# Running norms with another order, two norms joined, two modulation chunks and the forget gates' sums at other places

## The chip, the cores and the metric

The kernel runs on one core of a Trainium2 chip, in one launch. The metric is device time in microseconds. A core has TensorE (PE, matmuls), VectorE (DVE), ScalarE (ACT), GpSimd (POOL) and SyncE (SP, which here issues nearly all DMAs). Each engine works off its own queue in order, and the kernel orders them among each other by semaphores alone.

## The reference

Two blocks in a row, on 512 latent tokens of 1024 channels, and 256 context tokens in all but the last layer of the first block. All data is float32. Cut to what the change touches:

```python
def layer_norm(x, g, b):
    mu = jnp.mean(xf, axis=-1, keepdims=True)
    var = jnp.mean(jnp.square(xf - mu), axis=-1, keepdims=True)
    return (xf - mu) * lax.rsqrt(var + NORM_EPS) * g + b
...
for l in range(DEPTH):                                   # first_block, DEPTH = 2
    sh1, sc1, g1, sh2, sc2, g2 = split(silu_c @ w_mod[l] + b_mod[l], 6)
    a_lat = x_lat * (1 + sc1) + sh1
    m_lat, m_ctx = mixer(a_lat, a_ctx, ...)
    x_lat = layer_norm(ALPHA * x_lat + (1 + g1) * m_lat, ln1_g[l], ln1_b[l])
    f_lat = swiglu(x_lat * (1 + sc2) + sh2, ...)
    x_lat = layer_norm(ALPHA * x_lat + (1 + g2) * f_lat, ln2_g[l], ln2_b[l])
...
h = modulate(rms_norm_2(x, norm_mix), shift_m, scale_m)  # second_block, on x_lat
x = x + gate_m * hybrid_mixer(h, ...)                    # log_f = log_sigmoid(f_c + fox_bf); cum = cumsum(log_f)
h = modulate(rms_norm_2(x, norm_ffn), shift_f, scale_f)
x = x + gate_f * hierarchical_moe(h, ...)
```

After the last layer of the first block a layer norm and the second block's RMS norm follow each other with nothing between.

## The kernel before, in words

**Layout.** The stream x lies in SBUF with channels on the 128 partitions: 8 tiles of 128 channels, each 768 tokens wide (512 in layer 1). Sums over channels are matmuls with a matrix of ones.

**Dense pieces.** All large products go through `run_dense`. A piece is 128 output channels. SP loads its weights (`w_raw`, 8 or 11 blocks of 128x128), ACT rounds them to `w_hi` (L1217), DVE forms the rest `w_lo` (L1227), and PE adds w_hi by hi, w_lo by hi (L1200, L1201) and w_hi by lo (L1203). `w_raw`, `w_hi` and `w_lo` have two buffers each, so SP issues the load for piece n when w_lo of piece n-2 is done, and ACT casts it when PE has ended piece n-2. Per piece n every engine first prepares piece n+1, then does the background work registered for n (`behind`), then takes piece n's output. SP issues the load of a piece first and then the background work of the piece before.

**Background: modulation vectors.** `Vectors` computes silu(c) by w_mod beside a run of pieces: chunks of 512 columns, each in 4 steps. A step loads a quarter of the rows (`vec_w`, 512 KB, L930, two buffers; the next load waits until DVE has used the buffer), and DVE adds it up (L950, L953: 4 instructions for two vectors). Per chunk ACT and DVE split the sum (`vec_hi`, `vec_lo`, L979, L938) and PE puts it into a row of PSUM (L989). `start` is the piece at which it begins, `pieces` the number of pieces per chunk. In layer 0's projection (20 pieces) it computes 8 chunks, 2 pieces each, from piece 4: all vectors from column 2D on. In layer 0's feed-forward part (60 pieces) it computes layer 1's 12 chunks, 4 pieces each, from piece 2.

**Bias tables.** In the projections POOL gathers relative-position biases by 24 small DMAs in three groups of 8 (L1981) into a landing area and subtracts them from a mask (L1984).

**Norms.** A running norm (`Norm` with `running=True`) has its sums gathered while the dense layer in front still works: `Moments` centres x roughly (L1359), ACT squares it (L1371), POOL adds tiles up (L1378, L1382) and PE totals them (L1335). At the norm's start PE adds the last tile (L611), ACT makes minus the mean (L640), DVE and POOL subtract it (L736, 3 tiles; L750, 5 tiles), ACT loads the table with the square root and takes the root (L652, L654), DVE takes the reciprocal (L743) and multiplies (L768), ACT applies gain and modulation twice (L667: the rounded `ahi`, then the full value), and DVE forms `alo` (L773). Three norms are of this kind: both of layer 0 at width 768, and layer 1's first at 512. PE's first matmuls (L1178, L1179) interleave the first two pieces, so they need both their `w_lo` and one `ahi` tile at a time; L1184 follows with `alo`. The last norm of the first block is another function, `normalize`, in a block of its own: POOL has added the first seven tiles (L1305), PE sums (L486), DVE centres (L537), ACT squares and PE sums again (L502, L491), DVE, ACT and DVE make the reciprocal root (L540, L504, L542), DVE multiplies (L554) and ACT applies gain and bias (L515). The second block's norm then squares again (L649, L623), makes its own root (L758, L663, L760), and goes on as L768, L667, L773.

**Second block's projection.** 16 pieces with `Branches` behind them: convolution, gates, and the forget gates: softplus on DVE, a running sum `fox_cum` on DVE in piece 5 (L2769), then in piece 6 PE turns it (L2659) and spreads it over partitions (L2663), ACT copies it to `fox_ck` (L2705), DVE to `fox_cq` (L2776), and POOL makes the decay tables (L2827, L2831).

## Time and profile before

| what | us |
|---|---|
| median of 3 runs (lowest, highest) | 3197.33 (3195.94, 3199.88) |
| profiled execution: time | 3194.6 |
| profiled execution: span of the core | 3192.8 |
| PE busy | 2899.0 (91%) |
| DVE, ACT, POOL busy | 1684.6, 1231.2, 485.9 |
| mean granted TensorE clock | 0.953 |

The span reaches from the first to the last instruction of the core; the time of the execution has a little around it. "Busy" leaves out waiting. An engine that waits is followed by the name of what released it; a wait for several things is put down to the last of them. A granted clock of 1.00 is TensorE's upper level, 0.50 its lower.

### The profile page before, as it was taken

What the parts mean: (1) busy time and instruction counts of PE and PEld (TensorE: products, weight loads), DVE (VectorE), ACT (ScalarE), POOL (GpSimd) and SP (SyncE); (2) the same over time, 40 slices, a digit from 0 to 9 for tenths busy, and PEclk for the clock granted to TensorE, in tenths of its full rate; (3) what the DMA queues carried; (4) which work ended last, traced back from release to release, by engine and by line L of the source; (5) the groups of instructions that cost most, each with busy time, mean ns of one, the idle gap of its engine ahead of it and who ended that gap; (6) DMA issues with size and microseconds to landing.
All of it is one profiled execution on the core that took longest, in us unless ns stands there. A gap on an engine that the chain in (4) does not pass through costs nothing. (4 is left out here: it accounts for less than half of the span.)

```text
span 3192.8 us, 37028 instructions
## 1 busy us (share of the span) xinstructions
PE 2899.0 (91%) x14711; PEld 2304.0 (72%) x14711; DVE 1684.6 (53%) x2345; ACT 1231.2 (39%) x1827; POOL 485.9 (15%) x437
## 2 busy tenths in 40 slices
PE   7898899999979999999798799998999968876995
...
GB/s 208 150 185 32 24 1 38 62 70 60 52 40 131 128 122 107 120 91 41 99 60 16 24 10 99 99 83 114 190 165 190 93 32 81 159 76 192 371 241 79
DMA packets 397871, 330.11 MB, mean 103 GB/s; under 512 B 38038, under 2 KB 340484, under 8 KB 397572
## 3 DMA queue, kind: packets, MB, share of 16 engines
...
q10 hardware_dynamic: 256, 0.07, 0.0%
...
## 5 line engine op out<-in xcount | busy, mean ns | idle before, releaser
L1200 PE MATMUL ps<-ahi,w_hi 128*128 128x512 f32 (+1 forms) x2264 | 769.0, 353 | 11.2 <-DVE w_lo L1227 11.2
L1201 PE MATMUL ps<-ahi,w_lo 128*128 128x512 f32 (+1 forms) x2264 | 768.0, 353 | 0.0
L1227 DVE TENSOR_TENSOR w_lo<-w_raw,w_hi 128x1024 fp32r<-128x1024 f32 (+2 forms) x241 | 341.4, 1417 | 377.2 <-ACT w_hi L1217 375.3
L1200 PEld LDWEIGHTS ps<-ahi,w_hi 128*128 128x128 f32 x2264 | 428.9, 189 | 78.3 <-DVE w_lo L1227 14.6
L1203 PE MATMUL ps<-alo,w_hi 128*128 128x512 f32 (+1 forms) x2264 | 473.2, 351 | 0.0
L1217 ACT CAST w_hi<-w_raw 128x1024 fp32r<-128x1024 f32 (+2 forms) x244 | 285.7, 1171 | 485.3 <-PE ps L1203 368.4
L1201 PEld LDWEIGHTS ps<-ahi,w_lo 128*128 128x128 f32 x2264 | 429.0, 189 | 60.7 <-issue 0.2
L1203 PEld LDWEIGHTS ps<-alo,w_hi 128*128 128x128 f32 x2264 | 376.4, 189 | 58.0
L953 DVE SCALAR_TENSOR_TENSOR vec_acc<-vec_w,csilu,vec_acc 128x512 f32<-128x512 f32 x364 | 257.3, 752 | 8.3 <-DMA vec_w<-in_w_mod 3.6
L1290 DVE SCALAR_TENSOR_TENSOR x<-ps,mod,x 128x512 f32<-128x512 f32 x80 | 51.4, 668 | 241.8 <-PE ps L1203 226.9
L1378 POOL TENSOR_TENSOR xsum<-x 128x768 f32<-128x768 f32 (+1 forms) x3 | 5.1, 1692 | 1058.4 <-DVE x L1359 1058.4
L1200 PE MATMUL ps<-hhi,w_hi 128*128 128x512 f32 (+1 forms) x462 | 156.9, 354 | 0.0
L1201 PE MATMUL ps<-hhi,w_lo 128*128 128x512 f32 (+1 forms) x462 | 156.5, 353 | 0.0
L3342 ACT CAST e_hi<-e_raw 128x2048 fp32r<-128x2048 f32 x69 | 131.6, 1912 | 15.9 <-DMA e_raw<-in_w_up 9.7
L1898 POOL TENSOR_SCALAR prob<-prob,nm 128x512 f32<-128x512 f32 (+3 forms) x64 | 79.7, 1245 | 371.1 <-DVE nm L1823 371.1
L1452 ACT CAST hhi<-hf 128x768 fp32r<-128x768 f32 (+1 forms) x44 | 32.0, 727 | 268.6 <-DVE hf L1460 268.6
L1534 DVE TENSOR_TENSOR gp<-sg,ps 128x768 f32<-128x768 f32 (+1 forms) x32 | 26.3, 821 | 196.5 <-PE ps L1203 179.4
L1525 ACT ACTIVATE sg<-ps 128x768 f32<-128x768 f32 (+1 forms) x48 | 33.8, 705 | 241.0 <-PE ps L1203 241.0
L1263 ACT COPY proj<-ps 128x512 f32<-128x512 f32 (+2 forms) x58 | 40.0, 756 | 179.0 <-PE ps L1203 168.7
L2199 PE MATMUL ps<-mla_pt,proj 128*128 128x512 f32 x192 | 102.5, 616 | 0.0
L1200 PEld LDWEIGHTS ps<-hhi,w_hi 128*128 128x128 f32 x462 | 86.7, 188 | 13.2
L1201 PEld LDWEIGHTS ps<-hhi,w_lo 128*128 128x128 f32 x462 | 86.7, 188 | 12.8
...
## 6 DMA issues: line engine op xcount, KB each, us to landing
vec_w<-in_w_mod SPq DMA_DIRECT2D x128, 512.0 KB, 3.8
...
```

The costliest lines, as they stand in the source:

```text
L953: m = dve.scalar_tensor_tensor(out=acc, in0=w, scalar=f, in1=acc, op0=ALU.mult, op1=ALU.add)
L1200: pe.matmul(o, whi[:, j, b0 + b, :], hi[:, b, t0:t0 + tn], start=(b == 0), stop=False)
L1201: pe.matmul(o, wlo[:, j, b0 + b, :], hi[:, b, t0:t0 + tn], start=False, stop=False)
L1203: m = pe.matmul(o, whi[:, j, b0 + b, :], lo[:, b, t0:t0 + tn], start=False, stop=(b == nb - 1))
L1217: act.copy(whi[:, j, 0:d.blocks, :], raw_of(d, i, jj)).then_inc(hi_ready[j].sem, 1)
L1227: dve.tensor_tensor(wlo[:, j, 0:d.blocks, :], raw_of(d, i, jj), whi[:, j, 0:d.blocks, :].bitcast(F32), ALU.subtract).then_inc(lo_ready[j]. ...
L1263: m = act.copy(o_, s_) if scale is None else act.activation(o_, s_, ACT.Identity, scale=scale)
L1290: m = dve.scalar_tensor_tensor(out=xo, in0=ps[:, b + t0:b + t0 + tn], scalar=mod[:, v, bass.ds(i * 2 + (gate + jj), 1)], in1=xo, op0=ALU.m ...
L1525: act.activation(sg[:, jj, :], ps[:, 4 * BANK * jj:4 * BANK * jj + T], ACT.Sigmoid).then_inc(gated.sem, 1)
L1898: pool.tensor_scalar(self.prob[:, j, slot, 0:u.keys], self.prob[:, j, slot, 0:u.keys], self.nm[:, j, slot, 3:4], None, ALU.mult).then_inc( ...
L2199: m = pe.matmul(ps[:, bank:bank + LAT], weight(b, j), self.pt[:, s % 3, :], start=(b == 0), stop=(b == kt - 1))
L3342: act.copy(whi[:, n % HI, :], raw[:, n % RAW, :]).then_inc(e_hi.sem, 1)
```

## The change

Four edits.

1. In the three running norms the load of the table with the root moves to the end of the block before (`Moments.act`, at p == KT). ACT casts the first two weight pieces after the root instead of one before and one after it. DVE makes both `w_lo` after the first multiply; before, it made one ahead of the reciprocal, and POOL made the other between its subtractions.
2. `normalize` is gone. The last layer uses `Moments`, as the others do, and `DoubleNorm` computes layer norm and RMS norm in one block: it subtracts and multiplies, takes squares of gain times x plus bias on ACT, sums them on PE, applies gain and bias in place (6 tiles on DVE, 2 on ACT), takes the second root, and goes on as before. POOL makes both first `w_lo`.
3. In layer 0's projection `Vectors` computes 6 chunks from piece 8 on. The remaining 2 (the gate of the feed-forward part, from column 5D) come in layer 0's feed-forward part, in front of layer 1's 12 chunks, at 3 pieces per chunk instead of 4, in the same buffers.
4. The forget gates' turn and spread (PE), copies (ACT, DVE) move from piece 6 to piece 8.

```diff
-        def normalize(tiles, T, eps, gain, bias=None, center=False, post=None, after=None, src=None, presum=None):
...
-                    if center:
-                        dve.wait_ge(norm_mean.sem, norm_mean.base + 1)
-                        for k in range(n):
-                            dve.scalar_tensor_tensor(out=tiles[k], in0=ps[:, 0:T], scalar=-1.0 / dim, in1=src[k],
-                                                     op0=ALU.mult, op1=ALU.add).then_inc(norm_c.sem, 1)
-                    dve.wait_ge(norm_var.sem, norm_var.base + n)
-                    dve.tensor_scalar(rstd[:], ps[:, 1024:1024 + T], 1.0 / dim, eps, ALU.mult, ALU.add).then_inc(norm_rstd.sem, 1)
-                    dve.wait_ge(norm_sqrt.sem, norm_sqrt.base + 1)
-                    ch.link(dve.reciprocal(rstd[:], rstd[:]))
...
             def act_root(self, act):
-                act.activation(warm[:], ones[:, 0:1], ACT.Sqrt)
+                if self.tail:
+                    act.activation(warm[:], ones[:, 0:1], ACT.Sqrt)
                 act.wait_ge(*self.sem(norm_rstd, 1))
                 act.activation(self.rstd, self.rstd, ACT.Sqrt, bias=0.0 if self.tail else ln_eps[:]).then_inc(norm_sqrt.sem, 1)
 
-            def act_apply(self, act):
+            def act_apply(self, act, halves=None):
                 hi = self.post[0]
+                if self.running:
+                    halves(0)
+                    halves(1)
...
-                    if k == self.ON_DVE + 2:
-                        split(pool)
                     pool.tensor_tensor(self.src[k], self.src[k], self.sq[1], ALU.add).then_inc(norm_c.sem, 1)
...
                     if self.running and k == 0:
+                        halves(0)
+                        halves(1)
                         self.recentred(dve, 2)
...
+        class DoubleNorm(Norm):
...
+            def pe(self, pe):
+                pe.matmul(self.sums, ones[:], self.src[self.n - 1], start=False, stop=True, skip_group_check=True).then_inc(norm_mean.sem, 1)
+                pe.wait_ge(*self.sem(norm_sq, 1))
+                pe.matmul(self.squares, ones[:], self.sq[0], start=False, stop=True, skip_group_check=True).then_inc(norm_var.sem, 1)
+                for k in range(self.n):
+                    pe.wait_ge(*self.sem(norm_sq, k + 2))
+                    pe.matmul(self.sum2, ones[:], self.sq[k % 2], start=(k == 0), stop=(k == self.n - 1), skip_group_check=True).then_inc(norm_var.sem, 1)
...
+            ON_ACT = 6
+
+            def act_apply(self, act, halves):
+                for k in range(self.n):
+                    act.wait_ge(*self.sem(norm_x2[0], k + 1))
+                    if k >= 2:
+                        act.wait_ge(*self.sem(norm_var, k))
+                    act.activation(self.sq[k % 2], self.src[k], ACT.Square, scale=self.gain1(k), bias=self.bias1(k)).then_inc(norm_sq.sem, 1)
...
+                halves(0)
+                act.wait_ge(*self.sem(norm_rstd, 3))
+                act.activation(self.rstd, self.rstd, ACT.Sqrt).then_inc(norm_sqrt.sem, 1)
+                halves(1)
+                for k in range(self.ON_ACT, self.n):
+                    affine(k)
...
+            def recentred(self, dve, k):
+                dve.tensor_tensor(self.src[k], self.src[k], self.rest, ALU.add).then_inc(norm_x2[1].sem, 1)
+
+            def pool(self, pool, split):
+                pool.wait_ge(*self.sem(norm_g, 1))
+                for k in range(self.ON_DVE, self.n):
+                    pool.tensor_tensor(self.src[k], self.src[k], self.rest, ALU.add).then_inc(norm_c.sem, 1)
+                split(pool, 0)
+                split(pool, 1)
...
+            def dve_apply(self, dve, halves):
+                lo = self.post[1]
+                dve.wait_ge(*self.sem(norm_rstd, 2))
+                for k in range(self.n):
+                    dve.wait_ge(*(self.sem(norm_x2[1], k + 1) if k < self.ON_DVE else self.sem(norm_c, k - self.ON_DVE + 1)))
+                    dve.tensor_tensor(self.src[k], self.src[k], self.rstd, ALU.mult).then_inc(norm_x2[0].sem, 1)
+                    if k == 0:
+                        self.recentred(dve, 2)
+                for k in range(self.ON_ACT):
+                    dve.wait_ge(*self.sem(norm_sq, k + 2))
+                    dve.tensor_scalar(self.src[k], self.src[k], self.gain1(k), self.bias1(k), ALU.mult, ALU.add).then_inc(norm_mean.sem, 1)
+                dve.wait_ge(*self.sem(norm_var, self.n + 1))
+                dve.tensor_scalar(self.rstd, self.sum2, 1.0 / self.dim, self.eps, ALU.mult, ALU.add).then_inc(norm_rstd.sem, 1)
+                dve.wait_ge(*self.sem(norm_sqrt, 2))
+                dve.reciprocal(self.rstd, self.rstd).then_inc(norm_rstd.sem, 1)
+                dve.wait_ge(*self.sem(norm_rstd, 4))
...
+                def scaled(k):
+                    dve.wait_ge(*(self.sem(norm_mean, 2 + k) if k < self.ON_ACT else self.sem(norm_g, 3 + k - self.ON_ACT)))
+                    if k >= 2:
+                        dve.wait_ge(*self.sem(norm_tmp, k - 1))
+                    dve.tensor_tensor(self.xn[k % 2], self.src[k], self.rstd, ALU.mult).then_inc(norm_x2[0].sem, 1)
+
+                scaled(0)
+                scaled(1)
...
-            def __init__(self, c, w, cols, first, bias, dst, pieces, start=0, norm_first=False):
+            def __init__(self, c, w, cols, first, bias, dst, pieces, start=0, norm_first=False, end=6 * D, room=None):
                 self.cols, self.first, self.bias, self.dst, self.nv = cols, first, bias, dst, len(cols)
-                self.chunks = (6 * D - first) // self.CN
+                self.chunks = (end - first) // self.CN
...
+                if room is None:
...
+                self.room = self.raw, self.acc, self.hi, self.lo = room
...
@@ -1364,6 +1335,8 @@
                     dve.wait_ge(*self.at(self.centred, k + 1))
 
             def act(self, act, p):
+                if p == KT:
+                    act.activation(warm[:], ones[:, 0:1], ACT.Sqrt)
                 for k in self.SQUARED.get(p, ()):
                     act.wait_ge(*(self.at(self.centred, k + 1) if k <= 3 else self.written(k)))
...
@@ -2501,7 +2474,7 @@
                         if l == 0:
                             prologue(g["w_mod"][0], (0, 1), vec2[:, 0:48], mod, ring, w_in, proj, bt)
                         landing = proj[:, T_CQ:T_CQ + 3, :].rearrange("p a t -> p (a t)")[:, 0:ROWS * HEADS * 32].rearrange("p (r h c) -> p r h c", r=ROWS, h=HEADS)
-                        vectors = () if l else (Vectors(c1, g["w_mod"][0], (0, 1), 2 * D, vec2[:, 0:48], mod, 2, start=4, norm_first=True),)
+                        vectors = () if l else (Vectors(c1, g["w_mod"][0], (0, 1), 2 * D, vec2[:, 0:48], mod, 2, start=8, norm_first=True, end=5 * D),)
                         g0, b0 = (V_LN2_G + (l - 1) * KT, V_LN2_B + (l - 1) * KT) if l else (V_LN_IN_G, V_LN_IN_B)
                         norm = Norm(c1, xt(ALL), ALL, LN_EPS, lambda k, m=1: col(vec1, g0 + k, m), (ahi, alo, *modulate_by(mod, 0)),
                                     [proj[:, T_NV + n, :] for n in range(2)], proj[:, T_NV + 2, :], [proj[:, T_NV + n, :] for n in (3, 0, 1)],
...
-                           Vectors(c1, g["w_mod"][l + 1], (0, 1), 0, vec2[:, (l + 1) * 48:(l + 2) * 48], later, 4, start=2, norm_first=True))
-                room = vectors.raw[:].rearrange("p a b c -> p (a b c)")
-                moments = None if last else Moments(T, [room[:, n * T:(n + 1) * T] for n in range(2)], temps[0][:])
+                if last:
+                    vectors = (Vectors(c1, g["w_mod_2"][0], (2,), 0, vec3[:, 0:48], later, 4, start=2, norm_first=True),)
+                    vectors[0].ended()
+                else:
+                    gates = Vectors(c1, g["w_mod"][l], (0, 1), 5 * D, vec2[:, l * 48:(l + 1) * 48], mod, 3, start=2, norm_first=True)
+                    gates.ended()
+                    vectors = (gates, Vectors(c1, g["w_mod"][l + 1], (0, 1), 0, vec2[:, (l + 1) * 48:(l + 2) * 48], later, 3, start=gates.end, room=gates.room))
...
-            if last:
-                normalize(xt(T), T, LN_EPS, lambda k: col(vec1, g2 + k), lambda k: col(vec1, b2 + k), center=True, after=ALPHA, presum=xsum)
+                run_dense(new_ring(c1, NH), layers, moments.pool,
+                          background=(*vectors, moments.of(layers)), norm=norm)
+                moments.ended()
...
                     for t in range(4):
                         m = pe.transpose(ps[0:FOX_H, 6 * BANK + t * P:6 * BANK + (t + 1) * P], self.soft[:, 4 * t:4 * t + 4], ident[:])
                     m.then_inc(soft_rows.sem, 1)
-                if n == 6:
+                if n == 8:
                     pe.wait_ge(cum_done.sem, 1)
                     for t in range(4):
...
                         act.activation(self.a0[:, k, :], self.r[:, k, :], ACT.Exp, scale=self.sc[:, k:k + 1]).then_inc(a_exp.sem, 1)
                     for k in range(2):
                         act.activation(self.tmp[:, k, :], self.r[:, k, :], ACT.Tanh, scale=self.sc[:, 2 + k:3 + k]).then_inc(a_exp.sem, 1)
-                if n == 6:
+                if n == 8:
                     for h in range(FOX_H):
                         act.wait_ge(ck_mm.sem, h + 1)
                         act.copy(self.ck[:, h, :], self.bank(h)).then_inc(ck_copied.sem, 1)
...
-                if n == 6:
+                if n == 8:
                     dve.wait_ge(cq_mm.sem, 1)
                     dve.tensor_copy(self.cq[:], ps[:, 7 * BANK:7 * BANK + 16].rearrange("p (t h) -> p t h", h=FOX_H)).then_inc(cq_copied.sem, 1)
+                if n == 6:
...
+                            g2, b2 = V_LN2_G + (DEPTH - 1) * KT, V_LN2_B + (DEPTH - 1) * KT
+                            norm = DoubleNorm(c2, xt(LAT), LAT, lambda k: col(vec1, g2 + k), lambda k: col(vec1, b2 + k), RMS_EPS,
+                                        lambda k, m=1: col(vec1, V_MIX + k, m), (ahi, alo, *modulate_by(mod, 0)),
```

The names in the order below: w_raw and w_hi, w_lo are weight pieces, vec_w the modulation weights, x the stream, rstd the reciprocal root; a number at a name's end tells tiles apart. First SP's queue at the start of layer 0's projection, before and then after:

```order
L1124 UNCONDITIONAL_BRANCH
L1139 DMA w_raw<-in_w_in 128x8x128 x4
L930 DMA vec_w<-in_w_mod 128x2x512 x2
L1139 DMA w_raw<-in_w_in 128x8x128
L930 DMA vec_w<-in_w_mod 128x2x512 x2
```
```order
L1108 UNCONDITIONAL_BRANCH
L1123 DMA w_raw<-in_w_in 128x8x128 x8
L915 DMA vec_w<-in_w_mod 128x2x512 x2
L1123 DMA w_raw<-in_w_in 128x8x128
L915 DMA vec_w<-in_w_mod 128x2x512 x2
```

Eight weight loads (pieces 2 to 9) now stand in a row ahead of the first modulation load, where four stood. Next DVE's queue from the end of the first block to the second block's first pieces, before and after (the pairs L768, L773 go on the same way):

```order
L1290 SCALAR_TENSOR_TENSOR x<-ps,mod_9,x 128x512 x2
L1103 UNCONDITIONAL_BRANCH
L517 UNCONDITIONAL_BRANCH
L537 SCALAR_TENSOR_TENSOR x<-ps,x 128x512 x8
L540 TENSOR_SCALAR rstd<-ps 128x512
L542 RECIPROCAL rstd<-rstd 128x512
L554 TENSOR_TENSOR sq<-x,rstd 128x512 x8
L471 UNCONDITIONAL_BRANCH
L1222 UNCONDITIONAL_BRANCH
L704 TENSOR_TENSOR norm_co<-vec_4,mod_8 128x8
L708 COPY norm_co<-mod_8 128x8
L1227 TENSOR_TENSOR w_lo<-w_raw,w_hi 128x1024 x2
```
```order
L733 TENSOR_TENSOR x<-x,tmp_159 128x512
L611 SCALAR_TENSOR_TENSOR rstd<-ps,tmp_158 128x512
L733 TENSOR_TENSOR x<-x,tmp_159 128x512
L630 RECIPROCAL rstd<-rstd 128x512
L747 TENSOR_TENSOR x<-x,rstd 128x512
L733 TENSOR_TENSOR x<-x,tmp_159 128x512
L747 TENSOR_TENSOR x<-x,rstd 128x512 x7
L752 TENSOR_SCALAR x<-x,vec_4 128x512 x6
L754 TENSOR_SCALAR rstd<-ps 128x512
L756 RECIPROCAL rstd<-rstd 128x512
L763 TENSOR_TENSOR xn<-x,rstd 128x512 x2
```

One block less; the eight subtractions from PSUM are now three here and five on POOL, and both `w_lo` are gone from DVE. Last PE's queue at the forget gates, before (between pieces 5 and 6) and after (between pieces 7 and 8):

```order
L1203 MATMUL ps<-a2lo,w_hi 128x512 x8
L2659 MATMUL ps<-ident,fox_cum 128x4 x4
L2663 MATMUL ps<-fox_cum,fox_sel 128x512 x4
L1200 MATMUL ps<-a2hi,w_hi 128x512
L1201 MATMUL ps<-a2hi,w_lo 128x512
```
```order
L1187 MATMUL ps<-a2lo,w_hi 128x512 x8
L2631 MATMUL ps<-ident,fox_cum 128x4 x4
L2635 MATMUL ps<-fox_cum,fox_sel 128x512 x4
L1184 MATMUL ps<-a2hi,w_hi 128x512
L1185 MATMUL ps<-a2hi,w_lo 128x512
```

The same eight instructions stand two pieces later.

## Rows read from the trace of the kernel before

**Rows 1.** Timeline of layer 0's projection: start us, us, engine, line, operation [idle before <-releaser].
```profile
107.69 1.12 PE L1203 MATMUL ps<-alo,w_hi 128*128 128x256 f32 x8
116.03 1.12 PE L1203 MATMUL ps<-alo,w_hi 128*128 128x256 f32 x8
126.46 4.00 SPq L930 DMA_DIRECT2D vec_w<-in_w_mod  x2
128.46 6.05 POOL L1981 DMA_DIRECT2D proj<-rpb_rows  x8 [0.32 <-POOL na_bias L1984]
130.50 0.47 SPq L1139 DMA_DIRECT2D w_raw<-in_w_in  x1
147.64 7.87 POOL L1984 TENSOR_TENSOR na_bias<-na_mask,proj 128x256 f32<-128x256 f32 x8 [13.13 <-DMA proj<-rpb_rows]
148.66 1.04 ACT L1217 CAST w_hi<-w_raw 128x1024 fp32r<-128x1024 f32 x1 [12.99 <-DMA w_raw<-in_w_in]
153.22 0.61 PE L989 MATMUL ps<-vec_hi,pick_row 128*16 128x512 f32 x1 [10.12 <-DVE vec_lo L938]
159.17 0.43 PE L1200 MATMUL ps<-ahi,w_hi 128*128 128x512 f32 x1
```
**Rows 2.** Timeline of the second block's projection, around the forget gates.
```profile
2663.51 1.04 ACT L1217 CAST w_hi<-w_raw 128x1024 fp32r<-128x1024 f32 x1 [11.55 <-DMA w_raw<-in_w_in]
2666.99 0.59 PE L2659 MATMUL ps<-ident,fox_cum 4*128 4x4 f32 x4 [11.19 <-DVE fox_cum L2769]
2667.44 7.17 PE L2663 MATMUL ps<-fox_cum,fox_sel 4*128 4x512 f32 x8
2678.12 0.47 PE L1200 MATMUL ps<-a2hi,w_hi 128*128 128x512 f32 x1
2693.32 0.59 ACT L1263 COPY proj<-ps 128x512 f32<-128x512 f32 x1 [1.69 <-PE ps L1203]
```
**Rows 3.** PE's timeline from layer 1's last matmuls to the second block's first.
```profile
2557.88 2.68 PE L1203 MATMUL ps<-hlo,w_hi 128*128 128x512 f32 x11
2585.51 9.37 PE L623 MATMUL ps<-sq,ones 128*128 128x512 f32 x16 [12.75 <-ACT sq L649]
2603.97 0.77 PE L1178 MATMUL ps<-a2hi,w_hi 128*128 128x512 f32 x1 [9.09 <-ACT a2hi L667]
```
**Rows 4.** DVE's timeline in the same two norms.
```profile
2572.80 0.69 DVE L540 TENSOR_SCALAR rstd<-ps 128x512 f32<-128x512 f32 x1 [4.27 <-PE ps L491]
2574.19 3.35 DVE L542 RECIPROCAL rstd<-rstd 128x512 f32<-128x512 f32 x1 [0.70 <-ACT rstd L504]
2602.21 1.29 DVE L768 TENSOR_TENSOR xn<-x,rstd 128x512 f32<-128x512 f32 x2
```
**Rows 5.** Timeline of layer 1's running norm, width 512.
```profile
2171.92 1.10 PE L611 MATMUL ps<-x,ones 128*128 128x512 f32 x2 [0.30 <-PEq L1103]
2174.42 0.69 DVE L724 SCALAR_TENSOR_TENSOR sg<-ps,hf 128x512 f32<-128x512 f32 x1
2178.30 0.70 ACT L654 ACTIVATE sg<-sg,ln_eps 128x512 f32<-128x512 f32 x1
2182.42 1.70 DVE L768 TENSOR_TENSOR x<-x,sg 128x512 f32<-128x512 f32 x1
```
**Rows 6.** Timeline of layer 0's first running norm, width 768; the last row is width 512's.
```profile
924.12 2.82 DVE L1227 TENSOR_TENSOR w_lo<-w_raw,w_hi 128x1024 fp32r<-128x1024 f32 x1
936.85 8.50 ACT L667 ACTIVATE ahi<-x,norm_co 128x512 fp32r<-128x512 f32 x14 [2.04 <-DVE x L768]
...
2187.52 5.04 ACT L667 ACTIVATE ahi<-x,norm_co 128x512 fp32r<-128x512 f32 x7 [2.54 <-DVE x L768]
```
**Rows 7.** Weight tiles in layer 0's feed-forward part: time to landing.
```profile
DMA to landing us min/median/max: 3.6/3.9/5.5
```
**Rows 8.** That part's busy times (columns PE, PEld, DVE, ACT, POOL), and modulation chunks.
```profile
955.00:1440.00 485.00, 484.81 (x2767) 421.47 (x2768) 261.93 (x330) 112.52 (x121) 0.00 (x0) 0.99 0.39 115
...
L953 DVE SCALAR_TENSOR_TENSOR vec_acc<-vec_w,csilu,vec_acc x364: 737/746/1234, 104.2 to 2486.1; 128x512 f32<-128x512 f32 x182
```

191 lines of the change are left out of this document (52 added, 139 removed).

## The prediction

> **What bounds the kernel now.** I read the page first: PE is busy 91% of the span (the small table), so only two things can move the time: what PE has to do, and the stretches in which it waits. I then asked for PE's waits around the four edited places, and read the instructions in order of time in those stretches. Four waits come out. In layer 0's input projection PE stands still once for 10.12 us, and the page's releaser is the split of a modulation chunk [rows 1]. In the second block's projection it stands still for 11.2 us until a running sum is there [rows 2]. Between the last matmul of layer 1's feed-forward part and the first matmul of the second block, the chain runs through two whole norms [rows 3, 4]. And each of the three running norms has a gap of 11 to 14 us (the ends of the low halves and the reciprocal in [rows 5, 6]). The reader is to see that in all four the instruction PE waits for has itself waited: for a DMA, for a queue in front of it, or for a table load.
>
> **Layer 0's projection (term 1).** The wait at 143.10 (153.22 less 10.12) ends with vec_lo, but that split stands behind w_lo, w_lo behind w_hi, and w_hi waited 12.99 us for a weight load [rows 1]. That load was issued at 130.50 and its cast could start only at 148.66: 18.2 us, against 3.9 us (median to landing) where nothing is in the way [rows 7]. POOL had issued eight gathers of relative biases from 128.46 on, whose result was there at 147.64, so the load was caught behind them. It was issued that late because SP runs its queue in order, and in front of it stood modulation loads that wait until DVE has used the buffer: the pair at 126.46 goes out only after 4.00 us. The change takes the modulation loads out of the first four pieces. A piece lasts 8.34 us here (107.69 to 116.03, [rows 1]). Counting by that pitch from the end of piece 5 at 117.1 (116.03 and 1.12), pieces 6 to 9 would end at 125.5, 133.8, 142.1 and 150.5. The same load (piece 9's, pieces counted from 0) then goes out when w_lo of piece 7 is done, at about 120.3, and is needed as w_lo at 142.1. With 18.2 us to land and 2.4 us of cast and split it is ready at 140.9. Piece 10's load, at about 128.7, needs to be ready at 150.5 and is at 149.3. So even at the worst landing that this trace shows both are in time. What goes: 10.12 us of waiting, and the slow clock behind it. From 153.22 to 159.17 matmuls follow each other at 0.427 us, at the lower level, against 0.228 elsewhere (eleven in 2.68 us) [rows 1, 3]: 14 of them, 2.8 us. Term 1: 13.0 us saved; bounds 14 and 0 (the wait simply moves).
> The two chunks taken out go into layer 0's feed-forward part. Their 8 PE matmuls are moved, not added. There DVE gets 14 chunks in steps of 3 pieces instead of 12 in steps of 4. PE was busy 484.8 of 485 us in that stretch and DVE 261.9 [rows 8]; two more chunks are 32 instructions by 0.75 us, 24 us. Less the twelve chunks (192 by 0.746) DVE's own work is 118.7 us for 30 pairs of pieces, 4.0 a pair. Let all of it and two steps (8 by 0.75) fall into one piece, with 1.3 us of waiting for ACT between: 11.3 us. It starts 1.1 us after PE has ended the piece before, and with ACT's cast (1.04, [rows 1]) and its own low half (1.2) the next w_lo is done at about 14.7. PE needs it two pitches on, at 16.7. I cost this at nothing, with 2 us of cover per such piece.
>
> **The joined norms (term 2).** Before: PE's last dense matmul ends at 2560.56, the next real one starts at 2603.97: 43.4 us [rows 3] (2557.88 and 2.68, to 2603.97). After, the sums of layer 1's norm are gathered during the last layer as in the other running norms, and one chain remains. I build it from the running norm at the same width (512), from PE's start B (2171.92, [rows 5]). B comes 2.0 us after the last dense matmul, because two sums (twice the 1.10 us of this row) come first, as before that norm. DVE has the variance at B+3.2 and the second subtraction at B+4.15; the root ends at B+3.95, now without table load. Reciprocal 3.35: B+7.5. First multiply beside POOL 1.70, third subtraction 0.7, then seven multiplies by 0.70: DVE is through at B+15. Squares for the second norm start at B+9.3, PE's sums at B+10.1. Eight of them took 9.37 us in the old block [rows 3], so the sum stands at B+19.5. From variance to first multiply is 4.8 us and from there to PE's first matmul 1.76 us (2572.80 to the reciprocal's end, 2602.21 to 2603.97, [rows 3, 4]): PE starts at B+26.1. Casts, affine steps and POOL's two low halves lie beside the sums and the reciprocal. 2.0 + 26.1 = 28.1 instead of 43.4: 15.3 us saved. Against it stands one more pair of matmuls in the dense stream, 0.9 to 1.1 us [rows 5]. Term 2: 14.4 us; the DVE multiplies bound it: all eight at the contended 1.70 instead of 0.70 would give back 7, none contended would add 1, so 7 to 15.5.
>
> **The three running norms (term 3).** At width 512 the variance is ready at 2175.11, yet the root starts at 2178.30, behind a cast and the table load [rows 5]. The load moves to the end of the block before, where ACT is idle. So the reciprocal starts at about 2176.1 instead of 2179.0. But both low halves of the first weights now follow the first multiply on DVE (one stood on DVE before the reciprocal, one on POOL), and the third subtraction follows them. If DVE's instructions are slowed as the mean of the rows says, ACT's `ahi` row starts at 2185.0 instead of 2187.52 [rows 6]: 2.5 us. At width 768 the reciprocal was held by w_lo only (until 926.94 instead of 924.2), and the same row comes at 935.8 instead of 936.85 [rows 6]: 1.0 us, and 0.7 us in the other norm like it, where POOL's bias work follows sooner. Together 4.2. What speaks against it: the first w_lo took 2.82 us beside a POOL add [rows 6], where the same form alone takes 1.2. If the two new ones each wait for the POOL add in progress, w_lo starts one add (1.85) later, and what is left is 1.9 + 0.1 + 0.1 = 2.1. Term 3: 3 us saved, between the two; bounds 0 and 5.
> The Trainium skill (SBUF — State Buffer, "SBUF: two separate sides") says that the pair of ports that VectorE and GpSimd share is an exclusive lock: a VectorE instruction with two SBUF inputs against a reading GpSimd instruction blocks fully until the other ends. By that rule the sum would be 0.9 us worse, by the mean of the rows 1.2 us better.
>
> **The forget gates (term 4).** PE waits from 2655.8 to 2666.99, then runs the transposes and the eight matmuls for the decay (7.17 us, lower clock level), and only then piece 6, whose first nine matmuls are still slow: the clock rises at 2678.12, 11 us after work began [rows 2]. The wait itself stays: w_lo of piece 6 depends on the same late DMA and ends 1.2 us after that load's cast [rows 2], at 2665.8. But piece 6 now starts there. At 153.22 the clock rose 6.0 us after work had begun [rows 1]: 14 by 0.427, 10 by 0.228, piece 6 ends at 2674.1, piece 7 at 2679.6. The decay's matmuls then run at the full level in half the time, 0.3 + 3.5 us, and piece 8 ends at 2688.9 instead of 2693.3 [rows 2]. Term 4: 4.4 us saved; bounds 2 (piece 6 slow throughout) and 5. POOL's decay work ends about 7 us later in the queue, at about 2710; attention needs it after the projection's last piece, which lies some 40 us behind piece 8.
>
> **Sum.** 13.0 + 14.4 + 3 + 4.4 = 34.8 us. The profiled execution took 3194.6 us (span 3192.8), so 3159.8; the median of the runs is 2.7 us above it: 3162.5, and I say 3162.
>
> **Rivals.**
> (a) The late load stays late. The gathers also move: without modulation loads beside them they may be issued earlier and catch piece 9's load all the same, and piece 10's behind it. For it: one such load took 18.2 us. Against: margins of 1.2 us each at that worst case. By the Trainium skill (DMA: Bandwidth & Descriptors, "Queues, rings and completion order") a DMA engine takes turns between queues packet by packet, so a load should only be slowed beside gathers; the row of 18.2 us fits waiting behind them better. If the rival holds, 13 us are missing: 3175.
> (b) The joined norm is not much shorter: eight multiplies, eight squares and eight sums in a row, held by POOL's adds and a slow clock. For it: 1.70 against 0.70 us for a contended multiply [rows 4, 5]. Price 7 us: 3169.
> (c) Slower than before. Layer 0's feed-forward part becomes bound by DVE: the cover of 2 us in a two-step piece is gone if the multiply-adds run at their worst 1.23 instead of 0.75 us (8 by 0.48 is 3.9) [rows 8]. That is 1.9 us of waiting, and up to 2.9 us more if the clock falls each time, in 14 chunks: 67 us, so 3229. It turns the sign from 2.5 us per chunk on. Against: the projection of layer 0 does two steps in every piece without a wait after 165 us, and nothing contends with DVE in the feed-forward part.
>
> **How the numbers follow.** My forecast with all four terms: 0.72; (a) 0.12; (b) 0.09; (c) 0.04; 0.03 for something that ends near the old time. From no change I can tell about 0.2% (6 us). The forecast's own range is 3155 to 3169 (terms 2 to 4 at their bounds seldom together); to hold (a) and most of (b) the range is 3153 to 3177. Faster 0.93, same 0.03, slower 0.04.
>
> **What would show it.** Right: no wait above 2 us on PE between 84 and 250 us, the granted clock whole there; 28 us instead of 43 between layer 1's last dense matmul and the second block's first; second high halves 1 to 2.5 us nearer to the norm's start; decay matmuls of about 0.43 us after piece 7. Wrong: a wait for w_lo around 143 or 151 us, PE waits in the feed-forward part of layer 0, or the second norm's sum later than 22 us after the block's start.

## The result, and the profile after

The changed kernel took 3163.81 us (median of 3 runs, 3160.12 to 3168.68) against 3197.33 before. The ratio is 0.9900, with a 95% interval of 0.9876 to 0.9924. The forecast was 3162, in a range of 3153 to 3177. The profiled execution is the slowest of the three: 3168.7 us, with a span of 3166.9.

The clearest view is a table of milestones on PE, read from its waits in both traces (us from the start of the span). The last column is what the changed kernel is ahead by.

| PE's milestone | before | after | ahead |
|---|---|---|---|
| first matmul of layer 0's projection | 60.95 | 61.04 | -0.1 |
| first attention matmul of layer 0 | 302.29 | 288.48 | 13.8 |
| second pair of the first running norm | 938.21 | 921.78 | 16.4 |
| second pair of the second | 1527.45 | 1511.67 | 15.8 |
| second pair of the third | 2188.39 | 2168.53 | 19.9 |
| first matmul of the second block | 2603.97 | 2570.85 | 33.1 |
| its first attention matmul | 2737.51 | 2701.95 | 35.6 |
| first matmul of its output projection | 2814.78 | 2785.58 | 29.2 |
| end | 3192.8 | 3166.9 | 25.9 |

Layer 0's projection, timeline, as [rows 1]:

```profile
122.59 6.05 POOL L1954 DMA_DIRECT2D proj<-rpb_rows  x8 [0.32 <-POOL na_bias L1957]
...
128.76 0.37 SPq L1123 DMA_DIRECT2D w_raw<-in_w_in  x1
...
143.11 7.97 POOL L1957 TENSOR_TENSOR na_bias<-na_mask,proj 128x256 f32<-128x256 f32 x8 [14.47 <-DMA proj<-rpb_rows]
...
144.42 1.05 ACT L1201 CAST w_hi<-w_raw 128x1024 fp32r<-128x1024 f32 x1 [0.65 <-DMA w_raw<-in_w_in]
...
241.74 0.60 PE L972 MATMUL ps<-vec_hi,pick_row 128*12 128x512 f32 x1 [3.09 <-DVE vec_lo L922]
```

The load of piece 10 went out at 128.76, right behind the gathers, and was cast at 144.42: 15.7 us, nearly as long as the 18.2 before. But it was ordered early enough. PE's next wait over 0.8 us is the one at 241.74. Then layer 0's feed-forward part (busy time of PE, PEld, DVE, ACT, POOL, clock, DMA share, GB/s), and its modulation chunks, as [rows 8]:

```profile
939.00:1424.00 485.00, 484.12 (x2776) 420.27 (x2776) 286.27 (x368) 113.96 (x123) 0.00 (x0) 1.00 0.43 124
```
```profile
L937 DVE SCALAR_TENSOR_TENSOR vec_acc<-vec_w,csilu,vec_acc 128x512 f32<-128x512 f32 x196 | 134.6, 746 | 3.4 <-DVE vec_acc L937 3.4
```

DVE got the 24 us more that were forecast (286.27 against 261.93), and PE does not wait. The first running norm (width 768) and the third (512), as [rows 5, 6]:

```profile
905.38 11.05 POOL L635 TENSOR_TENSOR x<-x,vec_w 128x768 f32<-128x768 f32 x5 [8.75 <-ACT vec_w L523]
...
914.69 3.96 DVE L1211 TENSOR_TENSOR w_lo<-w_raw,w_hi 128x1024 fp32r<-128x1024 f32 x2
...
917.77 0.77 PE L1162 MATMUL ps<-ahi,w_hi 128*128 128x512 f32 x1 [12.02 <-DVE w_lo L1211]
...
921.78 0.79 PE L1162 MATMUL ps<-ahi,w_hi 128*128 128x512 f32 x1 [1.11 <-ACT ahi L554]
```
```profile
2165.54 0.76 PE L1162 MATMUL ps<-ahi,w_hi 128*128 128x512 f32 x1 [8.74 <-DVE w_lo L1211]
...
2168.53 0.80 PE L1162 MATMUL ps<-ahi,w_hi 128*128 128x512 f32 x1 [0.83 <-ACT ahi L554]
```

The first pair of tiles now waits for the low half, a wait that the prediction did not name. The pair behind it still waits for ACT. The joined norm, PE and DVE, as [rows 3, 4]:

```profile
2538.95 2.68 PE L1187 MATMUL ps<-hlo,w_hi 128*128 128x512 f32 x11
...
2543.65 1.10 PE L693 MATMUL ps<-x,ones 128*128 128x512 f32 x2 [0.30 <-PEq L1087]
...
2553.96 10.33 PE L698 MATMUL ps<-sq,ones 128*128 128x512 f32 x16 [8.36 <-ACT sq L714]
...
2569.10 1.29 DVE L763 TENSOR_TENSOR xn<-x,rstd 128x512 f32<-128x512 f32 x2
...
2570.85 0.77 PE L1162 MATMUL ps<-a2hi,w_hi 128*128 128x512 f32 x1 [6.56 <-ACT a2hi L730]
```

From 2541.63 to 2570.85 are 29.2 us instead of 43.4. And the second block around the forget gates, as [rows 2], with three stretches of the windows view (its first column behind the busy times is the granted clock):

```profile
2630.73 1.04 ACT L1201 CAST w_hi<-w_raw 128x1024 fp32r<-128x1024 f32 x1 [11.61 <-DMA w_raw<-in_w_in]
...
2633.08 0.80 PE L1184 MATMUL ps<-a2hi,w_hi 128*128 128x512 f32 x1 [10.45 <-DVE w_lo L1211]
...
2646.70 3.67 PE L2635 MATMUL ps<-fox_cum,fox_sel 4*128 4x512 f32 x8
```
```profile
2646.50:2650.50 4.00, 4.00 (x13) 1.78 (x14) 1.31 (x2) 3.28 (x6) 0.84 (x3) 1.00 0.75 94
2650.50:2655.00 4.50, 4.50 (x14) 3.54 (x14) 0.00 (x0) 2.83 (x3) 4.17 (x9) 0.62 0.89 119
2655.00:2658.00 3.00, 3.00 (x14) 2.43 (x13) 0.00 (x0) 0.25 (x1) 2.75 (x6) 1.00 0.29 42
```

PE's wait stands before piece 6, the decay's matmuls run at the upper level, and then the clock falls in piece 8. Last, the second block's attention, before and after, a stretch that no edit touches and in which 6.4 us are lost again:

```profile
2737.51:2814.78 77.27, 57.15 (x396) 32.09 (x397) 52.23 (x213) 53.21 (x189) 24.70 (x26) 0.89 0.49 184
```
```profile
2701.95:2785.58 83.63, 64.34 (x396) 35.84 (x397) 52.52 (x213) 53.16 (x189) 24.64 (x26) 0.79 0.45 170
```

The instructions are the same 396, the clock is 0.79 instead of 0.89.

### The profile page after: what moved, and what is told of

It is laid out like the page before. It is cut to its first block and busy times, and to the rows that moved or that the text cites. A ratio compares the mean times of both kernels' runs of the same rounds, so it can differ in the third digit from the quotient of the medians.

```text
span 3166.9 us, 37056 instructions
## 1 busy us (share of the span) xinstructions
PE 2902.4 (92%) x14705; PEld 2309.0 (73%) x14705; DVE 1684.1 (53%) x2358; ACT 1229.3 (39%) x1823; POOL 500.0 (16%) x447
## 5 line engine op out<-in xcount | busy, mean ns | idle before, releaser
L1184 PEld LDWEIGHTS ps<-ahi,w_hi 128*128 128x128 f32 x2264 | 427.6, 189 | 76.0 <-DVE w_lo L1211 13.3
L1498 ACT ACTIVATE sg<-ps 128x768 f32<-128x768 f32 (+1 forms) x48 | 33.8, 705 | 240.9 <-PE ps L1187 240.9
L1422 ACT ACTIVATE sg<-ps 128x768 f32<-128x768 f32 (+1 forms) x44 | 31.0, 705 | 168.6 <-PE ps L1187 168.4
```

The costliest lines, as they stand in the source:

```text
L1184: pe.matmul(o, whi[:, j, b0 + b, :], hi[:, b, t0:t0 + tn], start=(b == 0), stop=False)
L1498: act.activation(sg[:, jj, :], ps[:, 4 * BANK * jj:4 * BANK * jj + T], ACT.Sigmoid).then_inc(gated.sem, 1)
```

## The experiments

Ratios are to runs of the kernel before on the same chip, with their 95% intervals. They are wide for single edits, so the verdicts rest on the milestones. A milestone comes from one execution of each kernel, and two stretches that the edits hardly touch differ from trace to trace: attention in the second block, and layer 1, which takes 652.5 to 663.7 us from norm to norm in the 14 traces. Much of the latter is a wait of the same kind as term 1's, in the kernel before:

```profile
1548.54 5.29 POOL L1981 DMA_DIRECT2D proj<-rpb_rows  x7 [0.30 <-POOL na_bias L1984]
...
1564.48 1.04 ACT L1217 CAST w_hi<-w_raw 128x1024 fp32r<-128x1024 f32 x1 [7.14 <-DMA w_raw<-in_w_in]
...
1566.83 0.79 PE L1200 MATMUL ps<-ahi,w_hi 128*128 128x512 f32 x1 [4.69 <-DVE w_lo L1227]
```

A weight load of layer 1's projection is late beside a group of gathers. PE waits 2.5 to 5.2 us behind it in eleven traces, the changed kernel's (4.18) among them, and 1.6 or less in three, which have the shortest layer 1. That it is the gathers here too, and why the load is late in some executions and not in others, was not tested. For edits behind layer 1, the milestones are therefore counted from the third norm on.

**Each edit alone.** First the modulation chunks.

```diff
-vectors = () if l else (Vectors(..., mod, 2, start=4, norm_first=True),)
+vectors = () if l else (Vectors(..., mod, 2, start=8, norm_first=True, end=5 * D),)
+gates = Vectors(c1, g["w_mod"][l], (0, 1), 5 * D, ..., mod, 3, start=2, norm_first=True)
```

> The kernel before with the edit on the modulation chunks alone (6 chunks from piece 8 in layer 0's projection, 2 plus 12 chunks at 3 pieces each in its feed-forward part). Term 1 of the prediction: 13.0 us less. Nothing else may move: the three running norms start after 13.9, 13.9 and 11.3 us of waiting as before, the second block's gap stays 43.4 us. In the trace of the changed kernel the first attention matmul of layer 0 stands 13.8 us earlier, and the second running norm has given 1.6 us of it back, since the 8 matmuls of two chunks and their sums now stand in the feed-forward part. So I expect 12 to 13 us, 3184 to 3186. Rival (the gain hangs on the other edits, or the feed-forward part pays for it): under 6 us.

Ratio 0.9961 (0.9944 to 0.9977), median 3185.28. PE's timeline:

```profile
919.74 0.77 PE L1178 MATMUL ps<-ahi,w_hi 128*128 128x512 f32 x1 [13.94 <-ACT ahi L667]
...
1511.71 0.76 PE L1178 MATMUL ps<-ahi,w_hi 128*128 128x512 f32 x1 [13.86 <-ACT ahi L667]
```

The first running norm ends its wait 15.3 us sooner than before (935.01), the second 12.6 (1524.29). The feed-forward part between them gives 2.7 back. The 8 matmuls that moved there follow each other at 0.23 us and account for 1.9 of it. At layer 0's attention this kernel is 13.3 us ahead; at the third norm it is 10.0 (2175.22 against 2185.18), since layer 1, which the edit doesn't touch, took 2.6 longer. The net is 12.6 where layer 1 begins, the median's gain is 11.6: the theory holds. Then the joined norm.

```diff
-normalize(xt(T), T, LN_EPS, ..., center=True, after=ALPHA, presum=xsum)
+norm = DoubleNorm(c2, xt(LAT), LAT, ...)      # in the second block
+self.joined = last                            # table load at p == KT in the last layer only
```

> The kernel before with the joined norm alone (the table load moved for the last layer only; the other running norms, the chunks and the forget gates as before). Term 2: 14.4 us less. In the trace of the changed kernel the gap between the last dense matmul and the second block's first is 29.2 us instead of 43.4, and one more pair of matmuls of ones stands in the stream: 14.2 less 0.9 gives 13.3, so 3184. Rival (part of it comes from the other edits, since weights or sums are ready sooner): a gap of over 32 us and under 10 us gained.

Ratio 0.9955 (0.9940 to 0.9971), median 3182.34. From the third running norm's first matmul to the second block's first are 405.8 us (2177.41 to 2583.19), before 418.8: 13.0 less (expected 13.3), the gap itself is 29.5. The theory holds. The new order of the running norms:

```diff
-split(pool)                    # POOL's low half between its additions
+halves(0); halves(1)           # DVE, behind scaled(0)
+if p == KT: act.activation(warm[:], ones[:, 0:1], ACT.Sqrt)
```

> The kernel before with the new order of the three running norms alone. Term 3: 3 us less, bounds 0 and 5. The trace of the changed kernel, where PE's first matmul now waits for the low half and its second row of tiles for the rounded one, gives 1.0 us for each norm of width 768 and 2.7 us for the one of width 512: 4.7 in all. Expected in this trace: the same gaps (12.0, 12.0 and 8.7 us before the first matmul). In the median this is near what 3 rounds can tell. Rival (the gain at the start is lost to a later weight load, since the low half of piece 0 frees its buffer later): the norms' first pieces end no earlier than before.

Ratio 0.9977 (0.9959 to 0.9994), median 3188.71. From the end of the norm's last sum to its second pair are 16.0, 16.0 and 11.7 us; before 17.1, 17.0 and 14.5. That is 1.0, 1.0 and 2.8: 4.8 us. And the forget gates:

```diff
-if n == 6:
+if n == 8:
```

> The kernel before with the forget gates' turn and spread in piece 8 alone. Term 4: 4.4 us less, bounds 2 and 5: PE's wait of about 11 us stays and ends with the low half of piece 6, the decay's matmuls run in 3.5 instead of 7.2 us, and the stretch from piece 5's end to attention's first matmul gets 2 to 4.5 us shorter. The two traces so far show 2.4 us between the second block's first matmul and attention's first. Rival (what the forget gates no longer wait for is lost to the slow clock in piece 6, so that the sum is nothing): under 1 us.

Ratio 0.9995 (0.9981 to 1.0010), median 3196.53, which can't be told from no change. From the second block's first matmul to attention's first are 131.35 us (2606.22 to 2737.57), before 133.54: 2.2 us. Small as it is, it repeats: the five other traces with the gates' sums in piece 6 have 133.2 to 133.8 for this stretch, the changed kernel and the two others that differ from it only before this stretch 130.9 to 131.2. PE's wait before piece 6 is 10.2.

**Why the load was late.** The kernel before, with the third group of gathers held back.

```diff
+if b == 2 and late is not None:
+    pool.wait_ge(*late)        # piece 11's low half
```

> The kernel before, with the third group of eight gathers held back until piece 11's low half is there; modulation chunks from piece 4 as before. Theory (the weight load issued at 130.50 was caught behind the gathers): it now lands 4 to 6 us after its issue, its cast starts by 137, and PE's wait of 10.12 us at 143 is gone or under 1 us; about 13 us less, 3184. The gathers then catch a load of a later piece, whose cast may be late by a few us: up to 5 back. Rival 1 (the load is late because SP issues it behind modulation loads): the wait stays at 8 to 10 us. Rival 2 (the modulation loads themselves, 512 KB each, fill the queue in front of it): the load takes over 10 us without any gathers beside it.

Ratio 0.9974 (0.9960 to 0.9989), median 3187.44.

```profile
131.06 0.47 SPq L1139 DMA_DIRECT2D w_raw<-in_w_in  x1
...
137.35 1.05 ACT L1217 CAST w_hi<-w_raw 128x1024 fp32r<-128x1024 f32 x1 [0.73 <-DMA w_raw<-in_w_in]
...
157.54 6.05 POOL L1983 DMA_DIRECT2D proj<-rpb_rows  x8 [28.84 <-DVE w_lo L1227]
...
179.86 1.04 ACT L1217 CAST w_hi<-w_raw 128x1024 fp32r<-128x1024 f32 x1 [7.49 <-DMA w_raw<-in_w_in]
...
185.62 0.61 PE L989 MATMUL ps<-vec_hi,pick_row 128*16 128x512 f32 x1 [6.38 <-DVE vec_lo L938]
```

The same load, issued at the same time, is cast after 6.3 us instead of 18.2, and PE's wait at 143 is gone. The gathers catch the load of 164.08 instead, cast 15.8 us later, and PE waits 6.38 us there. So it is the gathers, wherever they stand. The Trainium skill (DMA: Bandwidth & Descriptors, "Queues, rings and completion order") has a DMA engine take turns between queues packet by packet, by which gathers should only slow a load. What these rows show is nearer to standing behind them: the loads that were issued next to the third group of gathers, in five traces, took 15.7 to 18.2 us to their cast. How the two queues share the DMA engines is not shown. Was it the later start or the fewer chunks that helped?

```diff
-mod, 2, start=8, norm_first=True, end=5 * D)
+mod, 2, start=4, norm_first=True, end=5 * D)
```

> The kernel before with the edit on the modulation chunks, but the 6 chunks of layer 0's projection begin at piece 4, as the 8 did before, and not at piece 8. It tells the fewer chunks from the later ones. Theory (the later start gives piece 9's load its place in SP's queue, ahead of the gathers' third group): with the start at piece 4 the modulation loads stand again in front of it, it is issued at about 130 behind the gathers, and PE waits 8 to 10 us at 143, as before; what is left of the gain is 1 to 2 us from the chunks' matmuls that moved, given back in the feed-forward part: 3195 to 3198. Rival (fewer chunks suffice): the wait is gone or under 3 us, about 3185.

Ratio 0.9971 (0.9956 to 0.9985), median 3187.63.

```profile
131.62 1.34 SPq L1139 DMA_DIRECT2D w_raw<-in_w_in  x1
...
149.68 1.05 ACT L1217 CAST w_hi<-w_raw 128x1024 fp32r<-128x1024 f32 x1 [14.01 <-DMA w_raw<-in_w_in]
...
153.76 0.60 PE L989 MATMUL ps<-vec_hi,pick_row 128*12 128x512 f32 x1 [10.66 <-DVE vec_lo L939]
```

The wait is back in full, so it is the later start that removes it. But more was gained than I expected (1 to 2 us): fewer chunks are worth something of their own. A second wait of the kernel before is gone, at the projection's end:

```profile
256.51 0.41 PE L989 MATMUL ps<-vec_hi,pick_row 128*16 128x512 f32 x1 [3.09 <-DVE vec_lo L938]
```

Six chunks from piece 4 end early, and PE need not wait for the last one; in the changed kernel that wait is still there (241.74). At layer 0's attention this kernel is 7.5 us ahead of the one before (294.77 against 302.29): 3.1 for that wait, 1.9 for the eight matmuls, and 2.1 for the sums behind them, which take 4.14 us at a clock of 1.00 instead of 6.20 at 0.66. The later start adds 5.8 there (288.95 in the kernel with the whole first edit), and 6.5 to 6.7 at the three norms: it takes away a wait of 10.7 us and brings that of 3.1 us at the end back. A start between pieces 4 and 8 might have had both gains; that was not tried. Against the kernel before, the milestones are 8.8 us at the first norm, 6.1 at the second and 3.3 at the third, where the median has 9. That its lead shrinks on the way is this execution's: it is the slowest of this kernel's eight, 7.5 us above their median, with the longest layer 1 of all traces (663.7 us).

**POOL's additions.** The changed kernel, four subtractions on DVE, four on POOL.

```diff
-ON_DVE = 3
+ON_DVE = 4
 self.recentred(dve, 2)
+self.recentred(dve, 3)
```

> The changed kernel, with four instead of three of the running norms' eight subtractions on DVE and four instead of five on POOL. In the changed kernel PE's first matmul waits for the first low half, which ends 1.1 to 1.3 us after POOL's last add (917.66 against 916.43, 2165.4 against 2164.21) though it had started 1.7 and 1.2 us before that end. Theory (a DVE instruction with two inputs in SBUF stands still until the POOL add that runs beside it ends): with POOL done one add sooner (2.2 us at width 768, 1.5 at 512) the low half takes its 1.2 us, and PE starts 1.7 to 2 us sooner in each norm; the later rows of tiles are held by DVE as before, so that 0 to 1 us per norm is left in the time. Rival (both share the port at a part of the speed, or the low half is long of itself): it still takes over 2 us and PE's start doesn't move.

Ratio 0.9881 (0.9858 to 0.9904), median 3160.11.

```profile
906.02 8.58 POOL L635 TENSOR_TENSOR x<-x,vec_w 128x768 f32<-128x768 f32 x4 [8.75 <-ACT vec_w L523]
...
915.34 2.35 DVE L1213 TENSOR_TENSOR w_lo<-w_raw,w_hi 128x1024 fp32r<-128x1024 f32 x2
...
916.96 0.77 PE L1164 MATMUL ps<-ahi,w_hi 128*128 128x512 f32 x1 [10.58 <-ACT ahi L554]
...
921.68 0.79 PE L1164 MATMUL ps<-ahi,w_hi 128*128 128x512 f32 x1 [1.82 <-ACT ahi L554]
```

Two low halves in 2.35 us instead of 3.96, with nothing changed but that POOL is done at 914.6. With five additions the first one ended 1.23 us after POOL's last, at both widths, however early it had begun. That is what the exclusive lock in the Trainium skill (SBUF — State Buffer, "SBUF: two separate sides") says, and the trace agrees: the one low half waits for the addition in progress (1.7 us), it isn't slowed. The rows show the other direction too: in the changed kernel's first norm, POOL's addition takes 1.79 us where DVE leaves the port alone and 2.5 where a DVE instruction got there first; and DVE's first multiply, which began at 913.67, some 0.3 us before an addition ended, took 1.10 us instead of 0.96. PE starts 1.4, 1.4 and 1.1 us sooner (expected 1.7 to 2), the second pair 0.7, 0.7 and 0.5: 2 us in all.

**The clock behind the decay's matmuls.** The changed kernel, operands of the spread filled with zeros to 128 partitions.

```diff
-self.cum = sb(c, "fox_cum", [FOX_H, LAT])
+self.cum = sb(c, "fox_cum", [P, LAT])
-self.sel = sb(c, "fox_sel", [FOX_H, FOX_H, P])
+self.sel = sb(c, "fox_sel", [P, FOX_H, P])
```

> The changed kernel, with the operands of the decay's spread (running sum and selector) filled up with zeros from 4 to 128 partitions; the eight matmuls compute the same. In the changed kernel they run at the full clock (3.67 us), and 0.8 us behind them piece 8's matmuls fall to the lower level for about 3.2 us, which costs the 1.9 us by which term 4 came out smaller (2.2 to 2.4 against 4.4). Theory (eight matmuls with 4 rows in the array count as little work for the clock): with 128 rows the clock stays, piece 8 takes 5.5 us instead of 7.2, and attention starts 1.5 to 1.9 us sooner, counted from the second block's first matmul. Rival (the fall comes from the wait before piece 6 or by chance): piece 8 takes 7.2 us again.

Ratio 0.9886 (0.9870 to 0.9903), median 3159.64. Timeline and windows:

```profile
2647.40 3.70 PE L2635 MATMUL ps<-fox_cum,fox_sel 128*128 128x512 f32 x8
```
```profile
2700.93:2778.12 77.19, 56.97 (x396) 32.18 (x397) 52.26 (x213) 53.27 (x189) 24.66 (x26) 0.89 0.49 185
...
2651.20:2655.70 4.50, 4.50 (x21) 3.65 (x20) 0.00 (x0) 2.87 (x3) 4.17 (x9) 1.00 0.85 118
```

As long as before, but behind them the clock stays at 1.00 where it was 0.62. The other traces agree: in all six with four rows in piece 8 the clock falls to 0.50 within 1.5 us behind these matmuls or already during them, in the two with 128 rows (this one and the last run) it does not fall. The stretch to attention is 129.4 us (2571.51 to 2700.93) instead of 131.1: 1.7 less. The theory that it is the four rows holds. The first row also answers another question: in this kernel, which has all four edits, attention takes 77.2 us at 0.89 again.

**Squares.** The changed kernel with four buffers for the joined norm's squares.

```diff
-act.activation(self.sq[k % 2], self.src[k], ACT.Square, ...)
+act.activation(self.sq2[k % 4], self.src[k], ACT.Square, ...)      # sq2 = [*sq, *xn]
```

> The changed kernel, with four instead of two buffers for the joined norm's squares (the two tiles of the scaled stream serve first as squares). In the changed kernel PE's sums over them take 10.33 us (9.37 predicted), ACT's squares wait for PE and PE for ACT in turn, though DVE has multiplied all eight tiles by 2558. Theory (the two buffers set the pace of 1.29 us a tile): ACT squares a tile in 0.72, PE sums one in 0.85 us, so the sum stands 2.5 to 3.5 us sooner and the gap of 29.2 us falls to 26 to 27. Rival (PE's lower clock alone sets it): 29 us as before.

Ratio 0.9899 (0.9882 to 0.9915), median 3166.44.

```profile
2557.47 3.78 PE L699 MATMUL ps<-sq,ones 128*128 128x512 f32 x4 [8.36 <-ACT sq L715]
2561.04 2.59 PE L699 MATMUL ps<-xn,ones 128*128 128x512 f32 x4
...
2565.18 1.88 PE L699 MATMUL ps<-xn,ones 128*128 128x512 f32 x4
```

From the norm's start to the second block's first matmul: 26.5 us instead of 27.2. My theory asked for 2.5 to 3.5 us and got 0.7: the first two tiles take 3.78 us, the last two 1.88, so for most of the sums PE's lower level after the wait sets the pace. But the buffers are not nothing. The sums take 10.28 to 10.66 us in the six traces with two buffers, 9.59 here and 9.94 in the last run with four.

**The next wait, before piece 6.** The changed kernel, SP's wait for the small loads put last.

```diff
     sp.dma_start(self.sinks[:], ...).then_inc(swa_in.sem, 16)
-    sp.wait_ge(swa_in.sem, 32)
+if n == 15:
+    sp.wait_ge(swa_in.sem, 32)
```

> The changed kernel, with SP's wait for the sliding-window bias and sinks (after piece 4's background) put at the end of the projection; its readers on DVE and POOL keep their own waits. In the prediction this wait blocks SP until the sinks have landed, so that the weight load of piece 6 goes out late and PE waits (10.45 us in the changed kernel, at 2633). Theory: the load is issued some 12 us sooner, PE's wait goes, with some 3 us of slow clock behind it: 10 to 13 us less than the changed kernel, 3151 to 3154. Rival (the queue of small DMAs in front of the load is what holds it, not SP): the load is issued sooner and lands at the same time; nothing gained.

Ratio 0.9880 (0.9855 to 0.9905), median 3161.65.

```profile
2627.01 1.04 ACT L1201 CAST w_hi<-w_raw 128x1024 fp32r<-128x1024 f32 x1 [6.16 <-DMA w_raw<-in_w_in]
...
2629.37 0.80 PE L1184 MATMUL ps<-a2hi,w_hi 128*128 128x512 f32 x1 [4.65 <-DVE w_lo L1211]
```

Half: the load goes out 6.2 us sooner (2611.84) and still takes 15.2 to its cast. PE's wait falls by 5.8 us, the stretch to attention by 2.8 (128.3). So SP's wait is one part of it. That the rest is what stands in the queue is argued here; the next two runs test it. The small loads themselves at another place:

```diff
-if n == 1:                     # 16 loads of the recurrence's weights
+if n == 2:
-if n == 4:                     # window bias and sinks
+if n == 8:
```

> The changed kernel with another order in SP's queue in the second block: the 16 small loads of the recurrence's gates one piece later (behind the weight load of piece 3), the window bias and sinks from piece 4 to piece 8 and the wait for them at the end. With the wait alone moved, PE's wait for piece 6 fell from 10.45 to 4.65 us and its load, though issued 6.2 us sooner, still took 15.2 us to the cast: small packets of the other loads stood in front of it. Theory (the weight loads lie behind a blocked SP and small packets): every cast from piece 3 on is in time, PE's wait before piece 6 is under 1 us, attention starts 9 to 13 us sooner after the second block's first matmul than in the changed kernel (131.1 us): 118 to 122. Rival (DVE's chain of the softplus, not the loads, holds the low halves): it stays over 126.

Ratio 0.9871 (0.9855 to 0.9888), median 3157.60. The stretch is 125.0 us, PE's wait 3.6. The theory had 118 to 122, the rival over 126, so neither is met in full. A load that follows the 16 small ones still comes late (8.0 us of waiting in ACT). At last all of it together, the small loads at the queue's start.

```diff
+sp.dma_start(self.bt[:], g["k_swa"]).then_inc(swa_in.sem, 16)      # at n == 0, with sinks and lru_w
-dve.memset(self.wbd[:], 0.0).then_inc(wbd_zero.sem, 1)             # at n == 0
+norm.ahead = lambda dve: dve.memset(branches.wbd[:], 0.0).then_inc(wbd_zero.sem, 1)
```

> The changed kernel with what the other runs point to: four subtractions on DVE in the running norms (2.0 us less in the traces), full rows for the decay's spread (1.7), four buffers for the squares (0.7), and in the second block all small loads (gates' weights, recurrence, window bias and sinks) at the start of SP's queue, right behind the first two weight loads, where the norm leaves the queue idle; the zeros that the recurrence's loads wait for are written before the norm. Theory (small packets and a blocked SP hold the weight loads): no cast waits for a DMA behind piece 2, PE's wait of 10.45 us before piece 6 is under 1 us, and with the slow clock behind it attention starts 13 us sooner after the second block's first matmul, and 1.7 us more for the full rows: 131.1 falls to 116 to 118. In all 15 to 18 us less than the changed kernel: 3146 to 3149, 0.985 of the kernel before. Rival 1 (DVE's background chain holds the low halves once the loads are in time, as the waits of 0.7 and 1.5 us in the last run hint): 120 to 124, 3151 to 3155. Rival 2 (the loads at the start delay the first pieces): the gap before the second block grows past 29.2 us.

Ratio 0.9830 (0.9813 to 0.9848), median 3143.08 (5 runs), where the changed kernel has 0.9900.

```profile
2565.00 0.77 PE L1169 MATMUL ps<-a2hi,w_hi 128*128 128x512 f32 x1 [6.56 <-ACT a2hi L737]
...
2613.98 0.50 PE L1191 MATMUL ps<-a2hi,w_hi 128*128 128x512 f32 x1 [1.58 <-DVE w_lo L1218]
...
2679.41 0.93 PE L1735 MATMUL ps<-swa_k,proj 64*128 64x128 f32 x8 [2.01 <-PEq L1094]
```

The stretch is 114.4 us instead of 131.1 (forecast 116 to 118), PE's longest wait in it 1.6. Of the 16.7 us, 1.7 belong to the full rows. Some casts still wait for their loads (4.6 us at the most), so "no cast waits" was too much; it costs PE almost nothing. Neither rival came: the gap before the second block is 28.8 us, no longer than in the changed kernel.

## Why the prediction was right, step by step

The time and its direction came as forecast, and each of the four edits gained for the reason that was given, though not to the size. By the single edits' traces the terms are:

| term | forecast | measured |
|---|---|---|
| 1, layer 0's projection | 13.0 | 12.6 |
| 2, joined norms | 14.4 | 13.0 |
| 3, running norms | 3 | 4.8 |
| 4, forget gates | 4.4 | 2.2 |
| sum | 34.8 | 32.6 |

That the median came within 2 us of 3162 is in part luck. The terms are off by 0.4 to 2.2 us each, one of them to the other side, the three executions lie 8.6 us apart, and up to attention in the second block the trace is 35.6 us ahead where the single edits add up to 32.6. Some 2.3 of the 3 us between were gained in layer 1 beyond what its norm explains (660.9 us between the second pairs before, 656.9 after), and layer 1 scatters by more than that.

**Term 1.** The weight load of piece 10 went out at 128.76 (forecast 128.7) and took 15.7 us (18.2 assumed), so the margin held. That the modulation chunks cost nothing in the feed-forward part was right, PE does not wait there, but the 2 us of cover were counted wrong: the stretch of [rows 8] holds 54 pieces and 168 of the multiply-adds, not 60 and 192. DVE's own work is then 5.1 us a pair and the cover about 1 us. It held all the same. I had written that the chunks' 8 matmuls were moved and then not booked them on either side: 1.9 us left the projection and 2.7 came back, near to cancelling. The whole term was put on the wait at 143. It is the largest part, but the chunks that left are worth 7.5 us at layer 0's attention by themselves, and the later start brought only 5.8 more, since the wait of 3.1 us for the last chunk stays. That wait stands in both traces (256.51 before, 241.74 after); I had overlooked it, and by my own sign, no wait above 2 us up to 250, it should not have been there.

**Term 2.** PE started 27.2 us after the norm's start, forecast 26.1. The step that was mis-sized is the sums over eight squares: 10.33 us for 9.37. I had taken the length from the old norm. The slow clock alone is not the difference, for the old norm's sums began at the lower level too: there it lasted 4.0 us, here 4.9. With two more buffers they took 9.59 and 9.94 us, so much of the excess is ACT and PE waiting for each other over two tiles, where ACT's square, now with gain and bias, takes 0.81 us instead of 0.63. How the rest divides is open. DVE's multiplies, which I let bound the term, were not slowed but for the first.

**Term 3.** The higher of my two readings (4.2) was nearer than the value taken between them. The reading against it, that both low halves wait for POOL, was true of the first one only, since POOL is through when the second begins, and the first holds the first pair and not the second, which decides. Width 768 gave 1.0 twice, as the mean of the rows had it, 512 gave 2.8 for 2.5.

**Term 4.** Up to the decay's last matmul all came as forecast: the wait stayed and moved to piece 6, pieces 6 and 7 ended 70.0 and 75.6 us after the block's first matmul (forecast 70.1 and 75.6), the spread took 3.67 us. Piece 8 then took 7.2 us instead of 5.5. The step that failed is that I let the clock stay up behind the eight matmuls, and with it 1.7 of the 2.2 us that are missing: the full rows brought as much back.

**The end.** The profiled execution lies 8.9 us above the 3159.8 forecast for it. Up to attention in the second block it is 35.6 us ahead, from there to the end it loses 9.7, at a lower clock in unchanged work. That stretch of attention took 77.2 to 83.6 us in the seven traces with all four edits and 77.1 to 81.7 in the seven without, so the change does not ask for it; what makes it differ from execution to execution is open. The other two runs, 3163.8 and 3160.1, enclose the forecast of 3162. The rivals: (a) had its cause right, gathers that hold a load, but the load was early enough; (b) came in part, 1.4 of its 7 us; (c) didn't come, DVE had 286 of 485 us and PE waited nowhere.
